# Four gate blocks of a modulation summed on VectorE during the second down-projection, in a one-core two-block transformer kernel

## The reference, cut to what matters

```
mod = silu(c) @ w_ada + b_ada                       # 1024 -> 6 * 1024
shift1, scale1, gate1, shift2, scale2, gate2 = split(mod, 6)
hn  = rms_norm(x, g_norm1) * (1 + scale1) + shift1
x   = x + gate1 * (mLSTM and block attention of hn @ w_in) @ w_out
hn2 = rms_norm(x, g_norm2) * (1 + scale2) + shift2
x   = x + gate2 * hierarchical_moe(hn2)             # 32 experts, top 2
out = rms_norm(x, g_final)
```

## Time and profile before

| | |
|---|---|
| time, median of 3 runs | 1361.96 us (1361.73 to 1362.55) |
| time of the profiled execution | 1362.35 us |
| its span, first to last instruction | 1360.5 us |
| mean granted TensorE clock | 0.995 |
| TensorE busy | 1326.2 us, 97% |
| VectorE busy | 768.3 us, 56% |
| ScalarE busy | 569.6 us, 42% |
| chain that ended last | PE 81%, DMA 8%, DVE 6%, ACT 3% |

### The profile page before, as it was taken

The page is one execution under the profiler, slowest core; times in us unless marked ns, Lnnn a source line. Parts: engine busy times, 40 slices in busy tenths (PEclk is TensorE's granted clock), DMA queues, the critical chain, the costliest instruction groups (busy, mean ns, idle before and its releaser), DMA issues.

```text
span 1360.5 us, 19453 instructions
## 1 busy us (share of the span) xinstructions
PE 1326.2 (97%) x7934; PEld 976.1 (72%) x7934; DVE 768.3 (56%) x1356; ACT 569.6 (42%) x858; POOL 33.7 (2%) x55
## 2 busy tenths in 40 slices
PE   8999999999999999999999999999999999999987
PEld 8988678999887998899988787764544454445442
DVE  5755477887787544698875877852322222222222
ACT  4344535555555477565554665541111111111123
POOL 2000000000001000000000000000000000000000
PEclk9999989999999999999999999999999999999998
DMA  9557266778866543255755563399999999999995
GB/s 340 189 195 264 95 227 223 245 239 278 308 234 219 171 163 123 72 186 185 247 191 179 189 236 124 124 406 396 428 428 427 428 429 428 429 427 427 428 421 212
DMA packets 113595, 372.83 MB, mean 274 GB/s; under 512 B 4572, under 2 KB 64252, under 8 KB 100592
## 3 DMA queue, kind: packets, MB, share of 16 engines
q1 hardware_dynamic: 105648, 344.07, 65.7%
q0 software_dynamic: 7872, 27.76, 5.9%
HBM read 370.75 MB, written 1.05 MB: 273 GB/s over the span
## 4 chain that ended last, share of the span: by engine, by line
PE 81%; DMA 8%; DVE 6%; ACT 3%; issue 1%; SPq 0%; ACTq 0%; DVEq 0%
PE ps L1545 14%; PE ps L659 12%; PE ps L621 8%; PE ps L622 8%; PE ps L623 8%; PE ps L1568 7%; PE ps L1527 4%; PE ps L636 3%; PE ps L638 3%; PE ps L637 3%; DMA arena<-in_w_expert_gate_dram 3%; DMA arena<-in_w_expert_down_dram 3%; DVE w_low L558 2%; PE ps L1574 2%; DMA arena<-in_w_ada_dram 1%; DMA ring<-in_ret_w_in_dram 1%
## 5 line engine op out<-in xcount | busy, mean ns | idle before, releaser
L558 DVE TENSOR_TENSOR w_low<-ring,w_high 128x1024 fp32r<-128x1024 f32 x264 | 311.4, 1221 | 121.0 <-ACT w_high L550 120.6
L550 ACT ACTIVATE w_high<-ring 128x1024 fp32r<-128x1024 f32 x264 | 264.9, 1052 | 199.6 <-PE ps L659 90.5
L621 PE MATMUL ps<-h_high,w_high 128*128 128x256 f32 x1088 | 311.8, 287 | 4.3 <-DVE w_low L558 2.3
L622 PE MATMUL ps<-h_low,w_high 128*128 128x256 f32 x1088 | 307.7, 283 | 0.0
L623 PE MATMUL ps<-h_high,w_low 128*128 128x256 f32 x1088 | 307.6, 283 | 0.0
L621 PEld LDWEIGHTS ps<-h_high,w_high 128*128 128x128 f32 x1088 | 208.4, 192 | 16.5 <-issue 8.2
L622 PEld LDWEIGHTS ps<-h_low,w_high 128*128 128x128 f32 x1088 | 208.6, 192 | 0.0
L623 PEld LDWEIGHTS ps<-h_high,w_low 128*128 128x128 f32 x1088 | 208.5, 192 | 0.0
L1545 PE MATMUL ps<-ring,arena 128*64 128x512 f32 x592 | 176.6, 594 | 2.5 <-DMA arena<-in_w_expert_gate_dram 2.0
L1545 PEld LDWEIGHTS ps<-ring,arena 128*64 128x64 f32 x592 | 56.4, 137 | 111.9 <-issue 111.7
L659 PE MATMUL ps<-w_high,h_high 128*128 128x512 f32 x304 | 95.7, 396 | 4.5 <-DVE h_low L574 3.6
(11 more groups left out here) (391 smaller groups left out, 1678.3 us busy)
## 6 DMA issues: line engine op xcount, KB each, us to landing
ring<-in_ffn_w_up_dram SPq DMA_DIRECT2D x44, 1024.0 KB, 7.7
ring<-in_w_expert_gate_dram SPq DMA_DIRECT2D x19, 2048.0 KB, 22.3
ring<-in_w_expert_up_dram SPq DMA_DIRECT2D x18, 2048.0 KB, 19.3
ring<-in_w_expert_down_dram SPq DMA_DIRECT2D x17, 2048.0 KB, 23.4
ring<-in_ret_w_in_dram SPq DMA_DIRECT2D x11, 2048.0 KB, 8.0
arena<-in_w_expert_up_dram SPq DMA_DIRECT2D x11, 2048.0 KB, 25.0
ring<-in_ffn_w_down_dram SPq DMA_DIRECT2D x10, 2048.0 KB, 9.4
arena<-in_w_expert_gate_dram SPq DMA_DIRECT2D x9, 2048.0 KB, 20.4
```

What stands on the lines that cost most here:

```text
L550: nc.scalar.activation(hi, raw, ACT.Copy).then_inc(hi_done, 1)
L558: last = eng.tensor_tensor(lo, raw, hi.bitcast(F32), ALU.subtract)
L621: nc.tensor.matmul(o, hi, hTh[:, k, :], start=(k == 0), stop=False)
L622: nc.tensor.matmul(o, hi, hTl[:, k, :], start=False, stop=False)
```

## The change

The gate blocks (places 8 to 11) are all summed on VectorE during down1, three steps in most halves, into accumulators in `hT` that are cleared beforehand and whose first row takes the bias by DMA. Their second weight buffer is `xn`. Places 5 to 7 are summed on VectorE in down0 as 9 to 11 were, and only places 3 and 4 stay on TensorE in up0. The sum over partitions of the eight other places moves from down0 to where `gate_sums(0)` stood, and that of the gates in front of the last half of down1, where ScalarE copies it to `gates`. Several waits move with them. A root on ScalarE is put behind the experts. Indentation is cut by eight in the diff and context is left out.

```diff
@@ -417,6 +417,7 @@
...
+    pe.wait_ge(ada_gate, 4)
@@ -709,11 +710,19 @@
...
 ada_w = [gates[:, :, :].rearrange("p a (b n) -> p (a b) n", n=C), carve(6656, 4, C)]
-ada_acc = carve(8704, 12 * C)
-NB = 12
-ADA_ROWS, ADA_PE = 3, 6
+NB, EARLY = 12, 8
+ADA_ROWS, ADA_PE = 3, 2
...
 msum = hT[:, 4:8, :].rearrange("p a b -> p (a b)")
+c_column = stat[:, 56:64]
...
+def ada_acc(place):
+    if place < EARLY:
+        return carve(8704 + place * C, C)
+    return hT[:, :, :].rearrange("p a b -> p (a b)")[:, (place - EARLY) * C:(place - EARLY + 1) * C]
...
+def ada_weights(place, kh):
+    return xn[:, :, :].rearrange("p a (b n) -> p (a b) n", n=C) if kh and place >= EARLY else ada_w[kh]
@@ -1002,25 +1011,31 @@
...
         nb = ADA_AT[place]
-        pool.dma_start(ada_w[kh], w_ada[:, 4 * kh:4 * kh + 4, nb * C:(nb + 1) * C]).then_inc(ada_in[kh], 16)
+        pool.dma_start(ada_weights(place, kh), w_ada[:, 4 * kh:4 * kh + 4, nb * C:(nb + 1) * C])\
+            .then_inc(ada_in[kh], 16)
...
     ada_load(0, 1)
-    for place in range(1, NB):
-        for kh in range(2):
-            pool.wait_ge(ada_used, 2 * place + kh - 1)
-            ada_load(place, kh)
-    pool.wait_ge(ada_used, 2 * NB)
-    for g, m in enumerate((2, 5)):
-        pool.dma_start(gates[:, g, :], A["b_ada_2"][0:1, m * D:(m + 1) * D].broadcast_to([P, D]))\
-            .then_inc(bias_in, 16)
+    def ada_loads(places):
+        for place in places:
+            for kh in range(2):
+                pool.wait_ge(ada_used, 2 * place + kh - 1)
+                ada_load(place, kh)
...
+    ada_loads(range(1, EARLY))
...
+    pool.wait_ge(ada_c, 2)
+    for g, m in enumerate((2, 5)):
+        pool.dma_start(hT[0:1, 4 * g:4 * g + 4, :].rearrange("p a b -> p (a b)"), A["b_ada_2"][0:1, m * D:(m + 1) * D])\
+            .then_inc(bias_in, 16)
+    pool.wait_ge(ada_used, 2 * EARLY)
+    ada_load(EARLY, 0)
@@ -1029,11 +1044,14 @@
...
     pool.dma_start(sel4[0:LH, :, :].rearrange("p a b -> p (a b)"), A["sel4"]).then_inc(mix_small, 16)
+    pool.wait_ge(norm_ss, NT * LATE)
+    ada_load(EARLY, 1)
...
     pool.dma_start(br[:, NG:], A["b_router_expert_2"][0:1, :].broadcast_to([P, NE])).then_inc(r_in, 16)
+    ada_loads(range(EARLY + 1, NB))
@@ -1126,68 +1144,61 @@
...
                 pe.wait_ge(up_free, i * 4 + ((FP + 4) * l + h + 1))
-                by_feature(h, buf, 2 * l + 1 if isinstance(i, int) and h == 0 else None).then_inc(wide_mm, 1)
-                if l == 0 and h % 2:
-                    pe.wait_ge(ada_in[h // 2], i * 16 + 16 * (ADA_ROWS + 1))
+                by_feature(h, buf, 2 * l + 1 if isinstance(i, int) and i == 0 and h == 0 else None).then_inc(wide_mm, 1)
+                if l == 0 and isinstance(i, int) and h % 2:
+                    pe.wait_ge(ada_in[h // 2], 16 * (ADA_ROWS + i + 1))
...
                     ada_part(4, h // 2)
-                if isinstance(i, int) and h == 1:
+                if isinstance(i, int) and i == 0 and h == 1:
...
         four(0)
-        with pe.Fori(1, 5) as i:
+        if l == 0:
+            four(1)
+        with pe.Fori(1 if l else 2, 5) as i:
...
             by_feature(h % 4, buf).then_inc(wide_mm, 1)
-            if l == 0:
-                pe.wait_ge(ada_in[h % 2], 16 * (ADA_ROWS + ADA_PE))
-                if h % 2 == 0:
-                    pe.wait_ge(up_free, 4 + 19)
-                ada_part(2, h % 2)
...
-        def last_ada(h):
...
+        def ada_evicted(h):
             if h == 0:
-                pe.wait_ge(ada_ev, ADA_PE)
-            if h == 1:
                 pe.wait_ge(ada_ev, 1 + ADA_PE)
-                pe.wait_ge(ada_used, 2 * (ADA_ROWS + ADA_PE))
-                pe.wait_ge(up_free, 4 + 20)
-                for half in range(2):
-                    for m in range(4):
-                        last = nc.tensor.matmul(ps[32 * m:32 * (m + 1), 2 + half, :], ones[:, 0:32],
-                                                ada_acc[:, m * D + half * C:m * D + (half + 1) * C],
-                                                start=True, stop=True)
-                last.then_inc(ada_mods, 1)
...
-        project(pe, f"down{l}", None if l else last_ada)
...
+        def gate_sums(h):
+            if h == count["down1"] - 1:
+                pe.wait_ge(ada_used, 2 * NB)
+                pe.wait_ge(up_free, 2 * (FP + 4))
+                for n in range(4):
+                    last = nc.tensor.matmul(ps[:, n, :], ones, ada_acc(EARLY + n), start=True, stop=True)
+                last.then_inc(ada_gsum, 1)
...
+        project(pe, f"down{l}", gate_sums if l else ada_evicted)
...
-    def gate_sums(g):
+    def modulation_sums():
         for half in range(2):
-            last = nc.tensor.matmul(ps[:, 4 + 2 * g + half, :], ones,
-                                    ada_acc[:, (4 + g) * D + half * C:(4 + g) * D + (half + 1) * C],
-                                    start=True, stop=True)
-        last.then_inc(ada_gsum, 1)
+            for m in range(4):
+                last = nc.tensor.matmul(ps[32 * m:32 * (m + 1), 4 + half, :], ones[:, 0:32], ada_acc(2 * m + half),
+                                        start=True, stop=True)
+        last.then_inc(ada_mods, 1)
     late_pe(pe, 2)
-    pe.wait_ge(ada_used, 2 * NB)
-    gate_sums(0)
+    pe.wait_ge(ada_used, 2 * EARLY)
+    modulation_sums()
...
         by_token(2 * (h // 2), buf, h % 2, 2 if h < 2 else None).then_inc(wide_mm, 1)
-        if h == 0:
-            gate_sums(1)
         if h == 2:
-            pe.wait_ge(ada_gate, 4)
+            pe.wait_ge(ada_ms, 2)
@@ -1741,8 +1752,7 @@
...
             act.wait_ge(ada_used, 2 * b + 2)
-            bank = 2 if b == ADA_ROWS + ADA_PE - 1 else 4
-            nc.scalar.activation(ada_acc[:, b * C:(b + 1) * C], ps[:, bank, :], ACT.Copy).then_inc(ada_ev, 1)
+            nc.scalar.activation(ada_acc(b), ps[:, 4, :], ACT.Copy).then_inc(ada_ev, 1)
@@ -1756,8 +1766,6 @@
...
                 src_high(act, f"down{l}", hff, 0, hff_ready(l))
-                if l == 0:
-                    ada_evict(ADA_ROWS + ADA_PE - 1)
@@ -1776,7 +1784,7 @@
...
             nc.scalar.activation(cv[:, n % 2, 0:T], cv[:, n % 2, 0:T], ACT.Silu).then_inc(up_si, 1)
-            if l == 0 and n % 4 == 3:
+            if l == 0 and n in (3, 7):
@@ -1785,16 +1793,14 @@
...
-        def ada_rest(h):
-            if h == 1:
-                act.wait_ge(ada_mods, 1)
-                nc.scalar.activation(msum[0:64, :].rearrange("p (n h k) -> p h k n", h=2, k=4),
-                                     ps[0:64, 2:4, :].rearrange("p h (k n) -> p h k n", k=4), ACT.Copy)\
-                    .then_inc(ada_ms, 1)
-                nc.scalar.activation(msum[64:128, :].rearrange("p (h n) -> p h n", h=2), ps[64:128, 2:4, :],
-                                     ACT.Copy).then_inc(ada_ms, 1)
...
-        project_act(act, f"down{l}", hff, hff_ready(l), 2, None if l else ada_rest)
+        def gate_rows(h):
+            if h == count["down1"] - 1:
+                act.wait_ge(ada_gsum, 1)
+                for n in range(4):
+                    nc.scalar.activation(gates[:, n // 2, (n % 2) * C:(n % 2 + 1) * C], ps[:, n, :], ACT.Copy)\
+                        .then_inc(ada_gate, 1)
...
+        project_act(act, f"down{l}", hff, hff_ready(l), 2, gate_rows if l else None)
@@ -1808,7 +1814,11 @@
...
+    act.wait_ge(ada_mods, 1)
+    nc.scalar.activation(msum[0:64, :].rearrange("p (n h k) -> p h k n", h=2, k=4),
+                         ps[0:64, 4:6, :].rearrange("p h (k n) -> p h k n", k=4), ACT.Copy).then_inc(ada_ms, 1)
+    nc.scalar.activation(msum[64:128, :].rearrange("p (h n) -> p h n", h=2), ps[64:128, 4:6, :],
+                         ACT.Copy).then_inc(ada_ms, 1)
@@ -2059,6 +2069,7 @@
...
         expert_end(0)
+    nc.scalar.activation(credit[:, 7:8], const[:, 0:1], ACT.Sqrt)
@@ -2158,14 +2169,14 @@
...
             kh, j = c // 4, c % 4
-            acc = ada_acc[:, place * C:(place + 1) * C]
+            acc, w = ada_acc(place), ada_weights(place, kh)[:, j, :]
+            column = cvec[:, c, 0:1] if place < EARLY else c_column[:, c:c + 1]
...
                 dve.wait_ge(ada_in[kh], 16 * (place + 1))
-            if c == 0:
-                ins = nc.vector.tensor_scalar(acc, ada_w[kh][:, j, :], cvec[:, c, 0:1], None, ALU.mult)
+            if c == 0 and place < EARLY:
+                ins = nc.vector.tensor_scalar(acc, w, column, None, ALU.mult)
             else:
-                ins = nc.vector.scalar_tensor_tensor(out=acc, in0=ada_w[kh][:, j, :], scalar=cvec[:, c, 0:1],
-                                                     in1=acc, op0=ALU.mult, op1=ALU.add)
+                ins = nc.vector.scalar_tensor_tensor(out=acc, in0=w, scalar=column, in1=acc, op0=ALU.mult, op1=ALU.add)
@@ -2233,8 +2244,12 @@
...
             pair(n)
-        steps = (0, 2, 5, 8, 11, 14, 17, 20, 24, 24, 24, 24)
-        project_dve(dve, f"down{l}", hff, None if l else lambda h: ada_rows(steps, h, ADA_ROWS + ADA_PE), 2)
+        if l:
```

(13 more changed lines are left out.)

## The result

The changed kernel takes **1371.99 us** (median of 4 runs, 1370.70 to 1374.87) against 1361.85 for the kernel before on the same chip: ratio 1.0077, 95% interval 1.0062 to 1.0091. The forecast was 1371.4 us, in a range of 1359.0 to 1376.0. Run once more later (`after_again`, 6 runs, expected 1370.5 to 1373.5), it took 1373.05 us, ratio 1.0078 (1.0065 to 1.0092).

What follows compares the result with a forecast made beforehand. It took the chain to run through TensorE in the projections and weights to bound the experts. -8.3 - 1.85 - 0.8 - 1.1 + 17.6 + 2.1 + 1.8 = +9.4 on 1362.0 gave 1371.4 us, range 1359.0 to 1376.0.

Steps and rivals of the forecast that it cites:

- seven parts less in up0: First up-projection: eight of twelve L1119 parts leave TensorE, the last worth nothing, 7 x 1.18 us: -8.3 us.
- L1160 leaves down0: First down-projection: this sum, 1.85 us in the chain, moves to where the first gate sum stood: -1.85 us.
- sb_v: In this stage the third half could start earlier; of TensorE's 1.4 us in hand, half is lost waiting: -0.8 us.
- small edits before up1: VectorE's clearing of hT and column copy fit in a 2.01 us wait: nothing; uncovered, up to 2.1 us.
- down1 at the full clock: Second down-projection: late block loads and four gate sums make half 10 end at 769.1 instead of 751.5: +17.6 us.
- norm behind it: After down1, ScalarE's four gate copies delay the mixing's w_high, then w_low and the residual: +2.1 us.
- low clock in down1 and the norm: After nearly 9 us without matmuls, clock 0.50 for 3.8 us, half of it lost: +1.8 us, bounds 0 and 1.9.
- end: Final root: its table is loaded once, saving a 1.28 us load for a dummy root of about 0.2: -1.1 us.
- ret_out, experts: No term of their own in the sum; experts, bound by weights, pass earlier shifts to the end one to one.
- Without late loads: Second down-projection with no block load late: its term is 7.7 us instead of 17.6.
- (3): Every load late, GpSimd held up under dense VectorE or two ring loads side by side: 1375.7 us, chance 0.12.
- (1): Block loads land alone, all taking 5.7 us, down1 term 7.7: -2.3 us, 1359.7 us, chance 0.17.

Runs made afterwards that it cites:

- e1: Changed kernel without the six late block loads (blocks 9 to 11; VectorE reuses place 8's weights), steps and sums kept: 1361.00 us, ratio 0.9994.
- v2: Changed kernel with two further buffers for the block loads (places 9 and 11), nothing left out: 1362.01 us, ratio 1.0003.
- e3: Changed kernel with seven idle turns on TensorE between half 9 and the wait for the gate sums: 1373.39 us, ratio 1.0084.
- after: The changed kernel itself, whole change against the kernel before: 1371.99 us, ratio 1.0077.
- e2: Changed kernel with four ring loads, issued just ahead of block loads, cut to a fraction: 1365.01 us, ratio 1.0020.
- e4: Kernel before with only the square root of a constant added behind the last expert pass's ScalarE work: 1361.69 us, ratio 1.0003.
- v3: Changed kernel with four block buffers, gate sums behind half 10, all copies on ScalarE, mix_in's first rounding after the norm's rows: 1351.47 us, ratio 0.9925.

## Why the prediction was right

The time, 1371.4 against 1371.99, and the mechanism are right: late block loads beside the ring's, VectorE through last, TensorE waiting, the sums in front of half 10. That the two times lie 0.6 us apart is in part luck. The change's own terms come to about +13 us in the trace, 24.3 less 11.3, against 9.4 forecast, and the medians rose by 10.1 and 10.9. Single terms:

| term | predicted | measured in the traces |
|---|---|---|
| seven parts less in up0 | -8.3 | -8.26 |
| L1160 leaves down0 | -1.85 | -2.13 |
| sb_v | -0.8 | -0.86 |
| small edits before up1 | 0 | 0 (shift -13.6 throughout) |
| down1 at the full clock | +17.6 | about +17.8 |
| norm behind it | +2.1 | +1.9 |
| low clock in down1 and the norm | +1.8 | about +4.6 |
| end | -1.1 | -0.5, lost again in the output's DMAs |
| ret_out, experts | 0 | -2.3 and +1.8, in stages that the change leaves alone |

- *up0.* L1119 x96 became L1137 x32, and the shift grows by 1.18 us at each part that is gone, six times, and once more behind the loop. The seven times 1.18 and the eighth as nothing were right.
- *sb_v.* w_high of the third half came 2.5 us late against the rest, behind ScalarE's copies, and TensorE waited 0.39 us there.
- *down1.* VectorE's waits were 2.88, 4.44 and 3.89 us (forecast 3.4, 3.6, 4.2) at the steps named, and the contended loads took 8.8, 10.1 and 9.0 us (9.3 taken). It was through at 746.7, which is 760.3 in the times of before (760.1). TensorE stood for 1.0, 4.2 and 7.0 us (1.6, 3.7, 8.9): 12.2 instead of 14.2, because half 9 ran slowly and filled the gap. From the start of the sums, 746.80, the sums and half 10 at the full clock (3.44 + 5.44) would have ended at 755.68, which is 769.3 in the times of before: 17.8 late. Without late loads the term was to be 7.7, with 2.1 for the norm 9.8: e1 and v2 have 10.6 and 10.8, of which 1.6 and 1.8 us are slow sums (5.17 and 5.40 against 3.60).
- *The clock was mis-sized*, the term with the largest error. The prediction took one slow stretch of 3.8 us, +1.8. The clock fell already behind the 4.2 us wait: half 9 took 7.15 us instead of 5.45, but that cost nothing, for VectorE was through only 7 us after it. The sums took 6.1 instead of 3.44 (+2.65), half 10 5.87 (+0.4), and the tiles of the norm 5.38 instead of 3.84 (+1.5). Together 4.6, in the slowest of four executions; in a median one it is probably less (the four have mean granted clocks of 0.990 at 1374.87 us and 0.992 and 0.993 at 1370.70 and 1370.94), but no trace shows it. e3 shows its part of it: with TensorE kept busy, the stage costs 3.0 less in the trace. Why the tiles ran slowly in after, e2 and e3 (5.4 to 5.5 us), and in e1 and v2 behind the same turns not (3.84), stays open.
- *The end was mis-sized* too, at 1.1 for 0.5: a table load had covered the wait for a mean (e4).
- Of the rivals, (3) in its form "GpSimd held up under VectorE" fell with e2. (1), the loads land alone, is what v2 makes true by other means, at its 10.8 us.

## What to carry to other kernels

Idle time in the windows is room only if the transfers behind the new work come in time and its result isn't wanted at once. The free VectorE time of down1 took 32 steps for 1.6 us (v3), and for 24 us with the same steps fed through two single buffers and summed in front of the last half. Two repairs, worth 13.5 (buffers) and 9.9 us (place of the sums) each by itself in the traces, together with the rounding moved behind the residual (1.0), turned a loss of 0.8% into a gain of 0.75%. And a long wait of TensorE has to be priced with what runs behind it: here the eight matmuls took 1.6 us more behind a wait of 3.55 us, and 3.0 more behind one of 7.

## What the runs showed of the hardware

- Waits of TensorE of 3.55, 4.16, 4.66 and 7 us left the same eight matmuls at 5.2 to 5.4, 5.4, 6.6 and 6.6 us; waits of 0.26 and 0.77, or none, at 3.6 to 3.7. The clock in their windows was 0.69 (3.55 us), 0.50 (7 us) and 1.00 (0.26 us).
- GpSimd's 1 MB block loads landed in 5.5 to 5.7 us where the ring's loads were cut to 256 KB (e2), and in 7.9 to 10.1 us when one of 2 MB was issued just before them (after, v2).
- The same code before ret_out ran at clock 1.00 in 172 to 176 us in eight of thirteen traces and at 0.50 to 0.74 in five, with TensorE busy for 2.5 of the 4 us in all but one. The stage ended 0 to 1.0 us off the trace of before in the five, and 1.8 to 2.6 us ahead in the eight. A row of each kind, after and after_again:

```profile
172.00:176.00 4.00, 2.51 (x14) 1.87 (x13) 3.25 (x6) 2.67 (x5) 0.75 (x1) 1.00 0.77 252
```

```profile
172.00:176.00 4.00, 2.53 (x10) 2.06 (x10) 2.53 (x5) 2.67 (x5) 0.75 (x1) 0.50 0.68 238
```

Two executions of one kernel differ by such amounts. An effect of 3 us such as e3's shows between two marks inside a trace and not in the medians here; but a trace is one execution, and for the changed kernel it gave 2 to 3 us more than the medians.
